# Layer 1's heads and sample states inside the loop over its input columns; layer 0's heads two at a time on the array's halves

## The reference

```
s   = (q k^T) * exp(log_d - m_t);   num = s v + (q C) * w_inter;   den = sum(s) + w_inter * (q n)
h   = num / max(|den|, exp(-m_t))
C'  = decay * C + (v * w_k)^T k;    n' = decay * n + sum(k * w_k)
```

## Time and profile before

| | |
|---|---|
| three runs, us | 928.23, 934.86, 939.1 (median 934.86) |
| the profiled execution, us | 934.51; its span from first to last instruction 932.7 |
| TensorE busy in the span | 859.5 us, 92% |
| VectorE, ScalarE, GpSimd busy | 598.4, 429.8 and 245.0 us |
| mean granted TensorE clock | 0.91 of full |

### The profile page before, as it was taken

The page is one execution under the profiler, slowest core; times in us unless marked ns, Lnnn a source line. Parts: engine busy times, 40 slices in busy tenths (PEclk is TensorE's granted clock), DMA queues, the critical chain, the costliest instruction groups (busy, mean ns, idle before and its releaser), DMA issues.

```text
span 932.7 us, 17030 instructions
## 1 busy us (share of the span) xinstructions
PE 859.5 (92%) x6219; PEld 770.2 (83%) x6219; DVE 598.4 (64%) x924; ACT 429.8 (46%) x732; POOL 245.0 (26%) x208
## 2 busy tenths in 40 slices
PE   5998898788959999999999999879959999999996
PEld 3977777642649999999999999856639999999995
DVE  4579884630146988886557557364586888887542
ACT  6345345331026655555545335454245655554443
POOL 5089734301103222221100000521122322222010
PEclk9999889896559999999999999955689999999997
DMA  9859745668704655545566667204334556554531
GB/s 311 303 165 299 240 138 203 202 192 269 245 32 149 181 181 180 180 141 151 168 184 201 182 182 230 85 22 114 111 116 140 178 182 181 181 157 145 184 105 47
DMA packets 158278, 159.83 MB, mean 171 GB/s; under 512 B 15857, under 2 KB 140413, under 8 KB 158207
## 3 DMA queue, kind: packets, MB, share of 16 engines
q1 hardware_dynamic: 149880, 152.68, 52.4%
q10 hardware_dynamic: 7574, 4.79, 1.7%
q0 software_dynamic: 768, 1.64, 0.5%
HBM read 150.76 MB, written 8.50 MB: 171 GB/s over the span
## 4 chain that ended last, share of the span: by engine, by line
PE 83%; DVE 9%; ACT 3%; issue 2%; DMA 2%; SPq 1%; ACTq 0%; DVEq 0%
PE bank L1580 21%; PE bank L1581 21%; PE bank L1582 21%; DVE w_lo L1057 2%; PE bank L1741 2%; PE bank L1769 1%; PE bank L2026 1%; PE bank L1979 1%; DVE sc_all L1130 1%; DMA kv<-in_cache_v 1%; PE bank L1666 1%; PE bank L1759 1%; ACT w_hi L598 1%; PE bank L2001 1%; PE bank L1990 1%
## 5 line engine op out<-in xcount | busy, mean ns | idle before, releaser
L1057 DVE TENSOR_TENSOR w_lo<-w_raw,w_hi 128x1024 fp32r<-128x1024 f32 (+2 forms) x230 | 294.1, 1281 | 103.7 <-ACT w_hi L598 103.4
L598 ACT ACTIVATE w_hi<-w_raw 128x1024 fp32r<-128x1024 f32 (+2 forms) x230 | 227.8, 992 | 245.6 <-PE bank L1582 243.4
L1580 PE MATMUL bank<-actB_hi,w_hi 128*128 128x264 f32 x704 | 200.1, 284 | 0.0
L1581 PE MATMUL bank<-actB_lo,w_hi 128*128 128x264 f32 x704 | 199.5, 283 | 0.0
L1582 PE MATMUL bank<-actB_hi,w_lo 128*128 128x264 f32 x704 | 199.3, 283 | 0.0
L1580 PE MATMUL bank<-actA_hi,w_hi 128*128 128x264 f32 x624 | 187.1, 300 | 2.8 <-DVE z L1548 1.6
L1581 PE MATMUL bank<-actA_lo,w_hi 128*128 128x264 f32 x624 | 182.0, 292 | 0.0
L1582 PE MATMUL bank<-actA_hi,w_lo 128*128 128x264 f32 x624 | 181.6, 291 | 0.0
L1581 PEld LDWEIGHTS bank<-actB_lo,w_hi 128*128 128x128 f32 x704 | 132.6, 188 | 0.1
L1580 PEld LDWEIGHTS bank<-actB_hi,w_hi 128*128 128x128 f32 x704 | 132.6, 188 | 0.1
L1582 PEld LDWEIGHTS bank<-actB_hi,w_lo 128*128 128x128 f32 x704 | 132.0, 187 | 0.0
(11 more groups left out here) (357 smaller groups left out, 1140.6 us busy)
## 6 DMA issues: line engine op xcount, KB each, us to landing
w_raw<-in_ffn_w SPq DMA_DIRECT2D x44, 1024.0 KB, 5.3
kv<-in_cache_k SPq DMA_DIRECT2D x64, 256.0 KB, 4.0
kv<-in_cache_v SPq DMA_DIRECT2D x64, 256.0 KB, 4.4
w_raw<-in_c_w_in SPq DMA_DIRECT2D x16, 1024.0 KB, 5.6
w_raw<-in_ab_w_in SPq DMA_DIRECT2D x14, 1024.0 KB, 6.9
w_raw<-in_ffn_w SPq DMA_DIRECT2D x16, 768.0 KB, 4.5
w_raw<-in_ffn_w SPq DMA_DIRECT2D x16, 640.0 KB, 4.1
w_raw<-in_ab_w_out SPq DMA_DIRECT2D x4, 1024.0 KB, 5.2
```

The source lines that it names most:

```text
L598: A(whi[u % RING][:, 0:nk, :], raw[u // 2 % RING][:, 0:nk, P * (u % 2):P * (u % 2) + P], ACT.Copy).then_inc(sem("hi_ready"), 1)
L1057: V.tensor_tensor(wlo[u % RING][:, 0:nk, :], raw[u // 2 % RING][:, 0:nk, P * (u % 2):P * (u % 2) + P], whi[u % RING][:, 0:nk, :].bitcast(F ...
L1580: M(bank[b][:, 0:T], hi[:, k, :], src[0][:, k0 + k, :], start=first and k == 0, stop=False)
L1581: M(bank[b][:, 0:T], hi[:, k, :], src[1][:, k0 + k, :], start=False, stop=False)
```

## The change

Layer 1:

- The 34 units go in the order gates, then q, q, k, k, v, v of a pair of heads, four times, then o (`in1_tile`, and `in1_column` for the loads). The loop is unrolled, and its units use banks 0 and 1 alone instead of four banks in turn, so that unit `e` waits for the evacuation of unit `e - 2`.
- The heads and sample states are put behind the units: `head_m` and `head_s` of head `h` after unit 9 + 3h, `head_num` after 10 + 3h, `head_squares` after 12 + 3h. A pair's token rows are turned after units 6, 12, 18, 24 (keys) and 8, 14, 20, 26 (values, and the samples' rows).
- A sample's state is handled in two halves of four heads, so there are 16 turns `c_sample` of half the size: after units 16 to 23 the lower heads, after 28 to 33 the upper ones, with two of them at 30 and at 32. `CRING` is 6 half states in the place of the six page slots. The rows for the outer products have buffers of their own (`q3`, `k3`, `v3`) and are made at units 15 and 27 on ScalarE and VectorE.
- The gate rows are computed at unit 3; GpSimd does 16 half-size `c_decay`, and the samples' normaliser (`n_step`) after all of them. SP's queue alternates weight loads with state loads and stores; a store waits for the state's addition and stands in front of a later weight load. The last gate (`o1_gated`) is done in four parts.

Layer 0:

- Two heads at once: `attn_s` and `ret_s` issue one head on each 64-row half of the array, into banks 4 and 5; `pair_pv` issues two heads' products in turn on the two 64-column halves.
- The query broadcast reads a 64-row operand (`q40`: the row's high part in rows 0 to 7, its low part in rows 32 to 39) in the one-pass 32-bit type (fp32r) that the units use.
- The key products are shared: VectorE does 11 of 32 (`k_mult_own`, at unit 6 and the odd units to 25), GpSimd 21, and each on GpSimd waits for VectorE's `split_lo` or `k_mult_own` of its unit.
- Value pages are loaded between the last key pages, and the first four `v_quad` come inside the loop (units 21, 23, 25, 27). The order after the loop changes: retention pair by pair, all eight `state_update` in one go with four buffers, `ret_o` with K = 128 and two columns (32 matmuls in place of 64), 16 quads after the loop become 12, of which seven stand behind `ret_o`.
- The turns of the input x are all made before the loop, those of the convolution parameters at units 10 and 11. One load of an activation table in the prologue is left out. The first unit of the output projection takes its K tiles 4 to 7 first and waits for the samples' part only before tile 0 (`late`).

The core of the diff:

```diff
+SAMPLE_AFTER = {16 + _n: [_n] for _n in range(8)}
+SAMPLE_AFTER.update({28: [8], 29: [9], 30: [10, 11], 31: [12], 32: [13, 14], 33: [15]})
...
+PAGES = [("k", j) for j in range(24)]
+for _m in range(4):
+    PAGES += [("v", _m), ("v", _m), ("k", 24 + 2 * _m), ("k", 25 + 2 * _m)]
+for _m in range(4, 16):
+    PAGES += [("v", _m), ("v", _m)]
 KSLOTS = 6
...
+POOL_K, DVE_K = {}, {}
+for _u in range(6, 27):
+    if _u < 26 and (_u % 2 or _u == 6):
+        DVE_K[_u] = len(POOL_K) + len(DVE_K)
+    POOL_K[_u] = len(POOL_K) + len(DVE_K)
+V_AFTER = {21: 0, 23: 1, 25: 2, 27: 3}
...
+                if u in DVE_K:
+                    pool.wait_ge(sem("k_mult_own"), list(DVE_K).index(u) + 1)
+                else:
+                    pool.wait_ge(sem("lo_ready"), u + LOOK + 1)
...
-                    pe.wait_ge(sem("jobs_out"), 1)
-                    M(b[:, :], eye8[:, what[1]:what[1] + 1].to_broadcast([NB, P]), tks["qa"][:], start=True, stop=True
+                    pe.wait_ge(sem("q_rows"), 3)
+                    pe.wait_ge(sem("q_lo"), 1)
+                    M(b[:, :], pick0[:, what[1]:what[1] + 1].to_broadcast([64, P]), q40[:], start=True, stop=True
...
+            def pair_pv(out, v, c, p):
+                for a, t, first, last in ((0, 0, True, True), (128, 0, True, False), (256, 1, False, True)):
+                    for i in range(2):
+                        d = DA * (2 * c + i)
+                        to = min(a, 128)
+                        ins = M(out[64 * i:64 * i + 64, to:to + 128], v[:, t, d:d + DA], p[i][:, a:a + 128], start=first, stop=last)
+                return ins
...
                 for b in range(NB):
-                    ins = M(bank[RET_O_BANKS[q]][r, 8 * c + b:8 * c + b + 1], s0[c][r, b, :], zt("qb", c)[r, TP + b:TP + b + 1],
-                            start=True, stop=True)
+                    at = 16 * c + 2 * b
+                    ins = M(bank[2][0:64, at:at + 2], s0[c][:, b, :], qm[:, c, b, :], start=True, stop=True)
...
+            def c_sample(n):
+
+                claim(6, "c_added", n + 1)
+                pe.wait_ge(sem("v_masked"), n + 1)
+                for h in range(4):
+                    cols = slice(DC * h, DC * h + DC)
+                    ins = M(bank[6][:, cols], vm[n % 2][:, cols], k3[:, cols], start=True, stop=True)
+                ins.then_inc(sem("outer"), 1)
+                claim(5, "q_mult", n + 1)
+                row_bcast(bank[5][:, :], n % NB, q3[:]).then_inc(sem("q_b"), 1)
+
+
+            for e in range(34):
+                claim(e % 2, "evac1_done", e + 3)
+                unit(U_IN1 + e, e % 2, actA, ready=("norm_lo", 16) if e == 0 else None)
...
+                if e in (6, 12, 18, 24):
+                    pe.wait_ge(sem("evac1_done"), e + 2)
+                    token_job("k", (e - 6) // 6)
+                if e in (8, 14, 20, 26):
+                    pe.wait_ge(sem("evac1_done"), e + 2)
+                    token_job("v", (e - 8) // 6)
+                    sample_job((e - 8) // 6)
+                if at_head(e, 10) is not None:
+                    head_num(at_head(e, 10))
+                if at_head(e, 9) is not None:
+                    if e == 9:
+                        pe.wait_ge(sem("m_hi"), 3)
+                        pe.wait_ge(sem("m_lo"), 1)
+                    head_m(at_head(e, 9))
+                    head_s(at_head(e, 9))
+                if at_head(e, 12) is not None and at_head(e, 12) < H - 2:
+                    head_squares(at_head(e, 12))
+                for n in SAMPLE_AFTER.get(e, []):
+                    if n % NB == 0:
+                        pe.wait_ge(sem("rows_lo"), 3 * (n // NB) + 3)
+                    c_sample(n)
```

## The result

The changed kernel takes 875.57 us (median of 6 runs, 872.14 to 877.82) against 934.18 (6 runs, 928.23 to 939.1): a ratio of 0.9374, 95% interval 0.9334 to 0.9414. Forecast were 873 in a range of 840 to 905. The profiled execution took 873.98 us, its span 872.2.

What follows compares the result with a forecast made beforehand. The prediction took TensorE, busy 92% of the span, as the bound. From 934.5 us it took 16.5 (layer 0's input loop), 33 (its tail) and 12 (layer 1), making 873; forecast 855 to 883, range 840 to 905.

Steps and rivals of the forecast that it cites:

- The tail: Layer 0 after its input loop: 89.4 us becomes 56.5, a gain of 33 us, bounds 23 to 45.
- a sign of being wrong: Layer 0's tail: the prediction is wrong if its 33 us gain comes out under 20.
- Layer 0's loop: Layer 0's input loop: 9.5 us less TensorE work and 7 less waiting, a gain of 16.5, from 5 to 29.
- The scores: Layer 0's input loop: prompt scores of two heads on two row halves save 2.2 us, bounds 0 and 4.5.
- The term for waiting and the clock: Layer 0's input loop: idle time and lower clock cost 21 us together, 14 left after, 7 less.
- VectorE follows: Layer 0's input loop: VectorE, with eleven more multiplications and shorter low parts, needs about 121 us against 148 and fits.
- Layer 1: Layer 1: heads among units run at the full clock; net gain 12 us, from -6 to 27.
- the waits that I priced at 15: Layer 1's loop: new waits, including restarts, banks, sample turns and GpSimd's decays, add 15 us, bounds 0 and 33.
- Engines that take turns: Rival, layer 1's loop: in-order queues block each other, 27 us of waiting, no gain there, total 885; chance 0.15.
- A loop paced by pages: Rival, layer 0's input loop: pages set the pace, it stays at 165 us, 16.5 lost, total 890; chance 0.12.
- A tail that stays warm: Rival: tail stays warm, waits hidden; 11 us more gained in tail, 10 in layer 1, 6 in loop: 846; chance 0.15.
- The slower case: Rival, layer 1's loop: it falls to the lower clock, up to 119 us more, with all 992; chance 0.03.

Runs made afterwards that it cites:

- the three gains together: Changed kernel with layer 1's doubled sample turns apart, retention's first two weights before the last sums, and tail quads early: 856.67 us, ratio 0.918.

## Why the prediction was right, and where it wasn't

*The total* (873 for 875.57) was met, and each of the three stages moved the way it was forecast; the terms don't agree as well as the total does. The tail's 18.7 us are under the 20 that I had named as a sign of being wrong, and its 14 us too much were made up by the loop (7), layer 1 (3) and the boundary in the feed-forward (3.5). That they did so is luck.

*Layer 0's loop* gained 23.3, not 16.5. The broadcasts were right (5 us forecast, 5.1 measured). The scores gained 3.4 where I took 2.2 between 0 and 4.5, the products 4.5 where I took 5.6: that figure came from summing busy times, in which pipelined matmuls overlap (11 us, when the stretches from issue to issue make 7.7). The term for waiting and the clock was the one off in size: I put it at 21 us, 5 of them for the clock, and left 14. In the kernel before, TensorE was busy for 16.7 us of the loop at 0.50, so the clock cost 8.3 and the term was 24.7; after, it is 12.6 (7.5 of idle time, and half of 10.2 us at 0.50). That is 12 us gained, not 7.

I had put the 11.1 us ahead of the products down to ScalarE's copies of the probabilities. In two of the three waits the trace of the kernel before has another cause behind the copies: ScalarE waits for VectorE's norm of the probabilities (L1164), which stands behind a low part of 3.26 or 3.36 us beside GpSimd's products. The first of them, VectorE and then ScalarE:

```profile
105.59 3.26 DVE L1057 TENSOR_TENSOR w_lo<-w_raw,w_hi 128x1024 fp32r<-128x1024 f32 x1
...
109.39 0.15 DVE L1164 RECIPROCAL sm<-sm 128x2 f32<-128x2 f32 x1
```

```profile
109.58 0.80 ACT L700 ACTIVATE smx<-smx,sm 128x128 f32<-128x128 f32 x2 [1.19 <-DVE sm L1164]
```

Still it isn't shown that the gate took these waits away: the run without it has low parts of up to 3.27 us and no wait ahead of the products either. What did, the pairs or something else in the change, no run separates. What the gate is worth in the changed kernel is shown: without it the time in which nothing runs on TensorE is 13.95 us instead of 7.5 (from 21.31 to 168.62 us, counted as in the table), at other places (the longest, 3.3 us, for ScalarE), which is nearly all of what that loop lost; I had given the gate none of TensorE's time.

*VectorE follows* was true with a thin margin that my sum didn't show. I set 121 us against 148 for the whole stage; from 60 to 120 us it is busy 57.65 of 60 (the windows of 20 us, one of which is shown, add up to that). The gate is what keeps it there: without it 6.8 us are lost. The Trainium skill's rule of the shared port (SBUF — State Buffer, "Who interferes with whom") is borne out a second time: from the run without the gate to the changed kernel GpSimd's products went from 2821 to 2380 ns and VectorE's from 1901 to 1302, when they seldom start into each other. What the gate gives back is smaller than I said for the low parts (1403, not 1254 ns), as GpSimd's product of 2.4 us still reaches into some of them (the 9 above).

*The tail* gained 18.7, not 33, and this is the term that failed. I wrote that value pages no longer come last, and let 6 us of retention's pairs and quads stick out of the softmax. Both are wrong. From the loop's end until TensorE turns the samples' second softmax (187.03 us) I had 15.7 us, and it took 25.2; from the end of the variance chain to the projection I had 2.4, and it took 7.7. At the start TensorE waits 7.3 us for VectorE, whose queue stands behind a key page (shown: with the order changed on VectorE the tail is 4.4 us shorter); at the end the last four quads wait 7.0 us for their pages (shown: without the pages of the last three the tail is 5.5 us shorter, with an order that frees slots earlier 5.2). I counted quads behind `ret_o` as hidden, but a quad that is done late also frees its slots late, and the page three quads on starts only then. `ret_o` at one sweep of 6.9 us was right (6.92), and so was the variance chain (9.8 us for 9.7). That the mean clock would not rise was right too (0.69 in both), though not in every step: the squares took 1.98 us at the full clock, where I had 3.65.

*Layer 1* gained 14.6 in my boundaries, where I had 12. That its work is the same and only the clock changes holds: the prompt's numerators, states and normalisers (`head_num` without its products) took 21.2 us before and 12.6 after, for the same 96 records; no run takes these heads out of the loop again. Of the waits that I priced at 15 (TensorE's idle time in the loop is 9.5 us), the doubled sample turns were the large one, and I had them at 4.5: they cost 8.4, as I didn't price the unit at half clock behind each. Beside GpSimd's decays the low parts take 1317 ns on average, for 1254 before: with 35 of them some 2 us, within my 3; I had called GpSimd nearly always busy in layer 0's loop, where it was so for 89.4 of 164.7 us.

*The rivals.* Engines that take turns: only at units 30 and 32. A loop paced by pages: only at its very end. A tail that stays warm: not here (0.69), only with the three gains together (0.78). The slower case, a loop at the lower clock, didn't come: small matmuls among units leave the clock at 1.00.

## What to carry to other kernels

Moving small, dependent work among large matmuls pays by the clock rather than by the work; look then for the single places where TensorE still stands for 2 us, since the price there was nearly twice the wait (8.4 us for 4.6). An engine's busy share over a stage says nothing on the stretch that counts: read windows of a few units before calling an added 14 us hidden, and test from both sides, by adding and by taking away. With a ring of slots, the order of the consumers is the order of the loads: work put behind a long step doesn't hide, if the load three places on waits for its slot.

## What the runs showed of the hardware

The lower clock came in two ways behind waits of nearly the same length. In the first TensorE stood for 2.33 us, ran 2 us at the full clock, and only then went to half, in the middle of a unit, which took 4.70 us instead of 3.17; in the second it stood for 2.24 us and ran at half (granted clock 0.52) from the first matmul on, and the unit took 5.65. A VectorE subtraction of two 128x1024 operands takes 1.22 us, and 1.92 on average when it starts while GpSimd multiplies pages; in the run with all keys on GpSimd even instructions of 0.2 us took 2.3. And two heads' scores on the two row halves take half the time per record (107 ns for 214) in whatever order the two heads are issued, while products on column halves gain 0.27 us a pair from being issued in turn.
